# RWKV level solve: the second T1 bank is copied by VectorE, the first by ScalarE

## The chip, the cores and the metric

The kernel runs on one core of one Trainium2 chip, as one launch. The metric is the device time of that launch in microseconds (us). Before the change three runs took 2896.85, 2897.07 and 2900.86 us, median 2897.07.

## The reference, cut to what matters

The program is a two-block transformer over 1024 tokens of width 1024. The second block has a mixer of which one half is an RWKV-7 recurrence of 8 heads of 64 channels, written in the reference as a scan over tokens:

```
def step(state, inp):                       # state: (heads, 64, 64)
    r_t, w_t, k_t, v_t, a_t, b_t = inp
    sa = einsum('bhvk,bhk->bhv', state, a_t)
    state = state * w_t + sa[..., None] * b_t + v_t[..., None] * k_t
    return state, einsum('bhvk,bhk->bhv', state, r_t)
```

The kernel computes this in chunks of 64 tokens. In a chunk the term `sa` couples every token with all earlier ones; resolving this needs the inverse of a unit triangular 64x64 matrix for each head and chunk. The inverse is built by doubling: blocks of size 2, then 4, up to 64. One doubling is called a level, and there are five (`LEVELS = 5`). With X the inverse of the diagonal blocks so far and L the part of the matrix that joins neighbouring blocks, a level computes T1 = L·X and then adds X·T1 to X (and the transpose of the product to the transposed copy XT).

## The kernel before

The change is in the stage `stage_rwkv_pairs`. Heads are handled two at a time: pair c = 0..3. A pair has 8 tiles of 128 tokens, that is 16 chunks, for each of its two heads j = 0, 1. One head's 16 chunk matrices of 64x64 lie side by side in one PSUM bank of 128x512.

All engines follow one list of steps, `script`, each through its own function of the same name. For a pair c it is: `turn`, `A`, `AV`, then `level 1` to `level 5`, then `tail`. Behind level m comes at times a `fill` (a piece of an unrelated projection on TensorE, behind some of the levels 2 to 4 of pairs 1 to 3), and then a step of the front of the next pair: behind level 1 `proj r`, behind level 2 `proj k`, behind level 3 `proj v`, behind level 4 `small`, behind level 5 `sums`. The last pair has no such steps, only fills. Nothing is reordered: each engine works through its own functions in this order.

A level on the engines:

- TensorE: T1 for j = 0 and then j = 1 (L1836), 64 instructions in all, into two banks of `ringA`. Then for each j it waits until that T1 bank has been copied, and multiplies it with XT (L1844, L1847) into one or two banks of `ringD`. Level 5 has the second product only.
- ScalarE: copies both T1 banks into SBUF, j = 0 and then j = 1 (L2208). In the profile the tile T1 is named LX.
- VectorE: adds the products to Xm (L2353) and XT (L2356), in the order Xm0, XT0, Xm1, XT1.

`small` of the next pair turns two small products of TensorE (L1768) into decay and gate: ScalarE applies four sigmoids and a square (L2138, L2143), VectorE a chain of seven operations with a scan (L2282 to L2292). `sums`: TensorE multiplies the squares of ScalarE with a matrix of ones (L1777); ScalarE takes the root (L2150) and then exponentials (L2152 to L2155); VectorE takes the maximum with 1e-12, the reciprocal and further products (L2302 to L2318), with the adds of the tail (L2365, L2369) among them; its last operation writes `at`. `tail` uses the finished XT in TensorE's products L1869 and others. The next pair's `turn` needs `at` and k of this front: TensorE's second group of transposes (L1789, of k) waits for it.

A ring is a set of four PSUM banks with two counting semaphores, `full` and `free`. TensorE takes banks in a fixed order and waits until `free` has counted the use four banks earlier. Counting works only if the banks are given back in the order in which they were taken.

Of the kernel before, what the change touches and what calls it, by code (L numbers as in the profile page):

```python
# [857 lines left out]
class Forget:  # L858
# [49 lines left out]
    def biased(self, dve, link):  # L908
        V, ring, of = self.nc.vector, self.ring, self.set
        link(dve, V.memset(self.one, 1.0))  # L910
        for hf in range(NH):
            dve.wait_ge(ring.full, ring.nth(("f", hf)))
            V.tensor_scalar(self.z[:, hf * HALF:(hf + 1) * HALF], ring.bank(("f", hf))[0:FOX_HEADS, :], self.E.b_forget[:], None,
                            ALU.add).then_inc(ring.free, 1)
        dve.wait_ge(ring.free, ring.nth(("f", NH - 1)))
        V.tensor_scalar(self.low, self.z, 0.0, None, ALU.min).then_inc(of["logit"], 1)

    def sums(self, dve, link):
        V, of = self.nc.vector, self.set
        dve.wait_ge(of["logit"], 1)  # L920
        dve.wait_ge(of["log"], 1)

        link(dve, V.tensor_tensor(self.e, self.e, self.low, ALU.subtract))
        V.tensor_tensor_scan(self.z, self.one, self.e, 0.0, ALU.mult, ALU.add).then_inc(of["ncum"], 1)
# [571 lines left out]
LEVELS = 5  # L1496
# [115 lines left out]
def stage_rwkv_pairs(nc, E, A):  # L1612
# [13 lines left out]
    with ExitStack() as st:  # L1626
        NW = 2
        split = slice(IN_THREE[0], ND)
        w, w_lo = [], []
# [30 lines left out]
        h_hi = [E.sb("h_hi0", [P, S], F32R, ctx=st)]  # L1660
# [5 lines left out]
        abT, akT, rbT, rkT, Xm, XT, T1 = (E.sb(x, [P, 2, W], ctx=st) for x in ("abT", "akT", "rbT", "rkT", "Xm", "XT", "LX"))  # L1666
# [5 lines left out]
        ringA = Ring(E.banks[0:4], E.sem("rwA_full"), E.sem("rwA_free"))  # L1672
        ringD = Ring(E.banks[4:8], E.sem("rwD_full"), E.sem("rwD_free"))
# [7 lines left out]
        router_landed = E.sem("router_landed")  # L1681
        modT, modT_set, mod_moved = E.sb("modT", [2 * ND, P], ctx=st), E.sem("modT_set"), E.sem("mod_rows_moved")
        uv_landed, uv_stored = E.sem("w_uv_landed"), [E.sem(f"uv_stored{i}") for i in range(2)]
        S_ = {x: E.sem("rw_" + x) for x in ("rest", "kept", "sq", "cc", "front", "level", "exp1", "exp2", "exp3", "stored", "tanh", "rstore", "ab", "h_hi", "h_lo", "w_hi", "w_lo", "u_hi", "u_lo")}
        w_in = A["w_in_2"][0].rearrange("(c p) n -> p c n", p=P)
        win = w_in[:, :, 2 * GW:]
        KIND = "rkv"
# [11 lines left out]
        front = [("proj", "r"), ("proj", "k"), ("proj", "v"), ("small",), ("sums",)]  # L1699
# [22 lines left out]
        with nc.Block() as block:  # L1722

            @block.tensor
            def _(pe):
                def take(ring, key):
                    bank, free = ring.take(key)
                    wait(pe, ring.free, free)
                    return bank
# [13 lines left out]
                def proj(c, kind):  # L1743
                    m = 3 * c + KIND.index(kind)
                    pe.wait_ge(w_landed[m % NW], 16 * (m // NW + 1))
                    for hf in range(NH):
# [3 lines left out]
                        if hf == 0:  # L1750
                            pe.wait_ge(S_["w_lo"], m + 1)
                        if m == 0:
                            pe.wait_ge(S_["h_lo"], len(IN_THREE) * (hf + 1))
                        for i, d in enumerate(IN_THREE):
# [6 lines left out]
                def small_(c):  # L1761
                    pe.wait_ge(ringD.free, ringD.nth(("lora", 0, 1)))
                    pe.wait_ge(S_["tanh"], 1)
                    pe.wait_ge(small, 16 * E.n_small)
# [6 lines left out]
                def sums(c):  # L1771
                    if c == 0:
                        pe.wait_ge(masks_set, E.n_masks)
                    pe.wait_ge(S_["sq"], c + 1)
                    for hf in range(NH):
# [3 lines left out]
                def turn(c):  # L1779
                    for x, src in (("v", v), ("k", k), ("b", bt), ("a", at)):  # L1780
                        if x == "v":
                            pe.wait_ge(ringD.free, ringD.nth(("v", c, 1)))
                        if x == "k":
                            pe.wait_ge(S_["front"], c + 1)
                        for hf in range(NH):
# [13 lines left out]
                def fill_(*at_):  # L1799
                    for _ in range(fill.get(at_, 0)):  # L1800
# [6 lines left out]
                        if t == 0:  # L1807
                            pe.wait_ge(S_["u_lo"], q + 1)
                        for i, d in enumerate(IN_THREE):
# [20 lines left out]
                def level(c, m):  # L1830
                    for j in range(2):
                        pe.wait_ge(S_["level"], 2 * (LEVELS * c + m - 1) + j + 1)
                        pe.wait_ge(ringD.free, ringD.nth(("X", c, j) if m == 1 else ("dXT", c, m - 1, j)))
                        bank = take(ringA, ("T1", c, m, j))
                        for t, rows in chunks:
                            last = nc.tensor.matmul(bank[rows, of(t)], L[other(rows), m - 1, j, of(t)], Xm[other(rows), j, of(t)], start=True, stop=True)  # L1836
                        last.then_inc(ringA.full, 1)
                    for j in range(2):
                        pe.wait_ge(ringA.free, ringA.nth(("T1", c, m, j)))
                        to_X = take(ringD, ("dX", c, m, j)) if m < LEVELS else None  # L1840
                        to_XT = take(ringD, ("dXT", c, m, j))
                        for t, rows in chunks:
                            if m < LEVELS:
                                last_X = nc.tensor.matmul(to_X[other(rows), of(t)], XT[rows, j, of(t)], T1[rows, j, of(t)], start=True, stop=True)  # L1844
                                if t == NT - 1 and rows.start:
                                    last_X.then_inc(ringD.full, 1)
                            last = nc.tensor.matmul(to_XT[rows, of(t)], T1[rows, j, of(t)], XT[rows, j, of(t)], start=True, stop=True)  # L1847
                        last.then_inc(ringD.full, 1)
# [10 lines left out]
                def tail(c):  # L1859
# [43 lines left out]
                    for t in range(NT):  # L1903
                        for q, rows, j, o in of_tiles:
# [3 lines left out]
                    fill_("Yi", c)  # L1908

                steps = {"lora": lora, "proj": proj, "small": small_, "sums": sums, "turn": turn, "A": a_part, "AV": av, "level": level, "tail": tail,  # L1910
                         "fill": fill_}
                for name, *args in script:
# [166 lines left out]
            def _(act):  # L2079
                def got(key):  # L2080
                    act.wait_ge(ringA.full, ringA.nth(key))
                    return ringA.bank(key)
# [117 lines left out]
                        nc.scalar.copy(aAV[:, j, :, HD:2 * HD], bank.rearrange("p (t n) -> p t n", t=NT)).then_inc(ringA.free, 1)  # L2200

                def level(c, m):
                    for j in range(2):
                        bank = got(("T1", c, m, j))
                        if not (c == 0 and m == 1):
                            before = (c, m - 1) if m > 1 else (c - 1, LEVELS)
                            act.wait_ge(ringD.full, ringD.nth(("dXT", before[0], before[1], j)))
                        nc.scalar.copy(T1[:, j, :], bank[:]).then_inc(ringA.free, 1)  # L2208

                def tail(c):  # L2210
                    for j in range(2):
# [17 lines left out]
            def _(dve):  # L2229
# [116 lines left out]

                def level(c, m):
                    V = nc.vector
                    for j in range(2):
                        if m < LEVELS:  # L2350
                            key = ("dX", c, m, j)
                            dve.wait_ge(ringD.full, ringD.nth(key))
                            V.tensor_tensor(Xm[:, j, :], Xm[:, j, :], ringD.bank(key)[:], ALU.add).then_inc(ringD.free, 1)  # L2353
                        key = ("dXT", c, m, j)
                        dve.wait_ge(ringD.full, ringD.nth(key))
                        V.tensor_tensor(XT[:, j, :], XT[:, j, :], ringD.bank(key)[:], ALU.add).then_inc(ringD.free, 1)  # L2356
# [1264 lines left out]
def build_program(nc, A):  # L3621
    with ExitStack() as ctx:
# [97 lines left out]
        with ExitStack() as second:  # L3720
            E.w_hi = [E.sb(f"wr_hi{i}", [P, len(IN_THREE), P], F32R, ctx=second) for i in range(2)]
            E.uv_hi = E.sb("uv_hi", [P, len(IN_THREE), UVW], F32R, ctx=second)
            E.sb("w_lora_rest", [P, ND * (2 * LORA + GATE_LORA) - len(IN_THREE) * (2 * P + UVW)], ctx=second)
            E.bonus = E.sb("bonus", [P, NT, 2 * NPAIR], ctx=second)
            E.carry = E.sb("carry", [P, NPAIR, NC], ctx=second)
            E.ident2 = E.sb("ident2", [P, HD], ctx=second)
            E.xg = E.sb("xg", [GATE_LORA, S], ctx=second)
            E.rw = E.sb("rw", [P, ND, N_GROUPS + EXPERTS], ctx=second)
            E.rb = E.sb("rb", [P, N_GROUPS + EXPERTS], ctx=second)
            E.hT = E.xT  # L3730
            with ExitStack() as ahead:
                E.w_o = E.sb("w_o", [P, ND, D], ctx=ahead)
                E.ws = E.sb("ws", [P, GW // HD, P], ctx=ahead)
                E.gln_w, E.gln_b = (E.sb(x, [P, 512], ctx=ahead) for x in ("gln_w", "gln_b"))
                E.g2 = E.sb("g2", [GATE_LORA, RW], ctx=ahead)
                E.bs = E.sb("bs", [P, GW // HD], ctx=ahead)
            E.run(stage_rwkv_pairs, A)
            modulated.close()
            E.run(stage_mix, A, x2_rows, x3_rows, n3_rows, y_slots)
# [39 lines left out]
```

## Time and profile before

| | |
|---|---|
| median of three runs | 2897.07 us |
| the profiled execution | 2900.66 us, of which the span from the first to the last instruction is 2898.9 us |
| TensorE busy | 2780.6 us, 96% of the span |
| VectorE, ScalarE, GpSimd busy | 1764.8, 1278.9 and 561.5 us |
| mean granted TensorE clock | 0.987 of full speed |
| the level steps of the stage | from 1604.6 to 1990.4 us of the span |

TensorE is the busiest engine over the whole program, but what one step is worth is read from the stretch in which it runs: which wait ends last there. In the timelines, an engine's idle time ahead of an operation stands in brackets with what ended it; "issue" means that the profile shows no releaser.

### The profile page before, as it was taken

What the parts mean: (1) busy time and instruction counts of PE and PEld (TensorE: products, weight loads), DVE (VectorE), ACT (ScalarE), POOL (GpSimd) and SP (SyncE); (2) the same over time, 40 slices, a digit from 0 to 9 for tenths busy, and PEclk for the clock granted to TensorE, in tenths of its full rate; (3) what the DMA queues carried; (4) which work ended last, traced back from release to release, by engine and by line L of the source; (5) the groups of instructions that cost most, each with busy time, mean ns of one, the idle gap of its engine ahead of it and who ended that gap; (6) DMA issues with size and microseconds to landing.
All of it is one profiled execution on the core that took longest, in us unless ns stands there. A gap on an engine that the chain in (4) does not pass through costs nothing. (4 is left out here: it accounts for less than half of the span.)

```text
span 2898.9 us, 48471 instructions
## 1 busy us (share of the span) xinstructions
PE 2780.6 (96%) x19821; PEld 2178.4 (75%) x19821; DVE 1764.8 (61%) x2546; ACT 1278.9 (44%) x2069; POOL 561.5 (19%) x383
## 2 busy tenths in 40 slices
PE   8999999999999999999999999998799899999997
PEld 6877767777777777776766676778678788888884
DVE  2332263686565566666435364363885899999996
ACT  2111020222454444544224233232443788888883
POOL 2222232131222222222230110110000111111102
PEclk9999999999999999999999999999899999999999
DMA  5111121663211222213121021124573899999997
GB/s 178 41 40 47 67 80 65 194 215 124 66 54 57 59 59 59 59 44 117 66 79 37 28 70 31 62 66 155 175 237 146 321 390 398 402 395 393 396 387 293
DMA packets 232145, 445.61 MB, mean 154 GB/s; under 512 B 18256, under 2 KB 160096, under 8 KB 206608
## 3 DMA queue, kind: packets, MB, share of 16 engines
q1 hardware_dynamic: 224896, 426.07, 41.4%
q0 software_dynamic: 7056, 16.79, 1.6%
q8 instruction: 142, 2.33, 0.3%
q14 instruction: 51, 0.42, 0.0%
HBM read 389.78 MB, written 61.94 MB: 156 GB/s over the span
## 5 line engine op out<-in xcount | busy, mean ns | idle before, releaser
L1223 DVE TENSOR_TENSOR fox_pT_lo<-psum,fox_pT_hi 128x512 fp32r<-128x512 f32 (+2 forms) x192 | 107.1, 558 | 180.2 <-ACT fox_pT_hi L1162 170.6
L1030 PE MATMUL psum<-x_hi,w_hi 128*128 128x512 f32 x512 | 210.7, 412 | 2.3 <-PEq L100 1.7
L1032 PE MATMUL psum<-x_hi,w_lo 128*128 128x512 f32 x512 | 200.9, 392 | 0.0
L1031 PE MATMUL psum<-x_lo,w_hi 128*128 128x512 f32 x512 | 200.2, 391 | 0.0
L3237 POOL DMA_INDIRECT xg<-n_rows,idx x33 | 84.5, 2562 | 476.2 <-PE psum L3124 454.3
L3347 DVE TENSOR_TENSOR lo_g<-land_g,hi_g 128x2048 fp32r<-128x2048 f32 x68 | 152.8, 2288 | 16.8 <-ACT hi_g L3273 16.8
L1173 ACT ACTIVATE fox_p<-fox_p,fox_bias 128x256 f32<-128x256 f32 (+7 forms) x128 | 99.6, 778 | 118.4 <-DVE fox_bias L1209 115.1
L3347 DVE TENSOR_TENSOR lo_u<-land_u,hi_u 128x2048 fp32r<-128x2048 f32 x66 | 150.6, 2285 | 0.0
L3347 DVE TENSOR_TENSOR lo_d<-land_d,hi_d 128x2048 fp32r<-128x2048 f32 x64 | 143.7, 2289 | 0.0
L181 PE MATMUL psum<-x_hi,w_hi 128*128 128x512 f32 x352 | 138.4, 393 | 0.0
L182 PE MATMUL psum<-x_lo,w_hi 128*128 128x512 f32 x352 | 137.9, 392 | 0.0
L183 PE MATMUL psum<-x_hi,w_lo 128*128 128x512 f32 x352 | 137.6, 391 | 0.0
L730 PE MATMUL psum<-wo_hi,y_hi 128*128 128x512 f32 x320 | 131.5, 411 | 0.0
L2075 POOL TENSOR_TENSOR L<-abT,m_level 128x512 f32<-128x512 f32 x40 | 56.1, 1434 | 377.6 <-ACT abT L2192 377.1
L1749 PE MATMUL psum<-hT,wr 128*128 128x512 f32 x288 | 127.9, 593 | 0.0
L3273 ACT CAST hi_g<-land_g 128x2048 fp32r<-128x2048 f32 x68 | 126.1, 1903 | 2.4 <-DMA land_g<-in_moe_w_gate 2.4
L1162 ACT CAST fox_pT_hi<-psum 128x512 fp32r<-128x512 f32 (+2 forms) x192 | 86.0, 483 | 92.3 <-PE psum L1058 92.3
L1135 POOL CAST w_hi<-w_land 128x1024 fp32r<-128x1024 f32 x46 | 47.7, 1037 | 399.9 <-PE psum L1032 317.6
L731 PE MATMUL psum<-wo_lo,y_hi 128*128 128x512 f32 x320 | 125.1, 391 | 0.0
L732 PE MATMUL psum<-wo_hi,yT_lo 128*128 128x512 f32 x320 | 124.7, 390 | 0.0
L3273 ACT CAST hi_u<-land_u 128x2048 fp32r<-128x2048 f32 x66 | 122.4, 1903 | 1.0 <-DMA land_u<-in_moe_w_up 1.0
L3273 ACT CAST hi_d<-land_d 128x2048 fp32r<-128x2048 f32 x64 | 118.8, 1905 | 5.7 <-PE psum L3131 5.5
(582 smaller groups left out, 7407.7 us busy)
## 6 DMA issues: line engine op xcount, KB each, us to landing
land_g<-in_moe_w_gate SPq DMA_DIRECT2D x66, 1024.0 KB, 7.3
land_u<-in_moe_w_up SPq DMA_DIRECT2D x66, 1024.0 KB, 7.2
land_d<-in_moe_w_down SPq DMA_DIRECT2D x64, 1024.0 KB, 8.2
ada<-in_ada_w SPq DMA_DIRECT2D x24, 1024.0 KB, 5.3
y_slots<-yb SPq DMA_DIRECT2D x33, 512.0 KB, 9.3
w<-in_w_in SPq DMA_DIRECT2D x27, 512.0 KB, 4.0
wo<-in_w_out SPq DMA_DIRECT2D x12, 1024.0 KB, 10.7
w_land<-in_w_kv_shared SPq DMA_DIRECT2D x23, 512.0 KB, 4.1
```

What stands on the lines that cost most here:

```text
L181: self.nc.tensor.matmul(bank[:], hi[:, d, :], E.x_hi[:, d, cols], start=(d == 0), stop=False)
L182: self.nc.tensor.matmul(bank[:], hi[:, d, :], E.x_lo[:, d, cols], start=False, stop=False)
L183: last = self.nc.tensor.matmul(bank[:], lo[:, d, :], E.x_hi[:, d, cols], start=False, stop=(d == ND - 1))
L730: nc.tensor.matmul(bank, hi, w_hi, start=first, stop=False)
L731: nc.tensor.matmul(bank, hi, wo_lo[:, c, cols], start=False, stop=False)
L732: last = nc.tensor.matmul(bank, E.y_lo[:, c, rows], w_hi, start=False, stop=final)
L1030: nc.tensor.matmul(bank[:], hi[:, d, :], E.x_hi[:, d, cols], start=(d == 0), stop=False)
L1031: nc.tensor.matmul(bank[:], hi[:, d, :], E.x_lo[:, d, cols], start=False, stop=False)
L1032: last = nc.tensor.matmul(bank[:], lo[:, d, :], E.x_hi[:, d, cols], start=False, stop=(d == ND - 1))
L1749: nc.tensor.matmul(bank[:], w[m % NW][:, d, :], E.hT[:, d, cols], start=(d == 0), stop=False)
L3273: nc.scalar.copy(w_hi[kept_in(x, b)][:], land[kept_in(x, b)][:]).then_inc(hi_set[x], 1)
L3347: V.tensor_tensor(w_lo[kept_in(x, b)][:], land[kept_in(x, b)][:], w_hi[kept_in(x, b)][:].bitcast(F32), ALU.subtract).then_inc(lo_set[x], 1)
```

## The change

ScalarE copies T1 of j = 0 only. VectorE copies T1 of j = 1, as the first operation of its own `level` function, and counts it in a new semaphore `T1`. The bank of j = 1 is given back by VectorE, after it has waited until ScalarE gave back that of j = 0, so that the order holds. ScalarE ends its `level` with a wait for that. TensorE waits for the new semaphore ahead of the products of j = 1.

```diff
@@ TensorE, level(c, m) @@
                     for j in range(2):
-                        pe.wait_ge(ringA.free, ringA.nth(("T1", c, m, j)))
+                        if j == 0:
+                            pe.wait_ge(ringA.free, ringA.nth(("T1", c, m, 0)))
+                        else:
+                            pe.wait_ge(S_["T1"], LEVELS * c + m)
@@ ScalarE, level(c, m) @@
-                    for j in range(2):
-                        bank = got(("T1", c, m, j))
-                        if not (c == 0 and m == 1):
-                            before = (c, m - 1) if m > 1 else (c - 1, LEVELS)
-                            act.wait_ge(ringD.full, ringD.nth(("dXT", before[0], before[1], j)))
-                        nc.scalar.copy(T1[:, j, :], bank[:]).then_inc(ringA.free, 1)
+                    bank = got(("T1", c, m, 0))
+                    if not (c == 0 and m == 1):
+                        before = (c, m - 1) if m > 1 else (c - 1, LEVELS)
+                        act.wait_ge(ringD.full, ringD.nth(("dXT", before[0], before[1], 0)))
+                    nc.scalar.copy(T1[:, 0, :], bank[:]).then_inc(ringA.free, 1)
+                    act.wait_ge(ringA.free, ringA.nth(("T1", c, m, 1)))
@@ VectorE, level(c, m) @@
                     V = nc.vector
+                    dve.wait_ge(ringA.full, ringA.nth(("T1", c, m, 1)))
+                    V.tensor_copy(T1[:, 1, :], ringA.bank(("T1", c, m, 1))[:]).then_inc(S_["T1"], 1)
+                    dve.wait_ge(ringA.free, ringA.nth(("T1", c, m, 0)))
+                    dve.wait_ge(S_["T1"], LEVELS * c + m)
+                    dve.sem_inc(ringA.free, 1)
                     for j in range(2):
                         if m < LEVELS:
                             key = ("dX", c, m, j)
```

The new semaphore is also added to the table `S_` at the head of the stage.

## Rows read from the trace of the kernel before

**Rows 1.** Busy time by stretch: us; PE, PEld, DVE, ACT, POOL busy; PEclk; DMA.
```profile
1627.00:1661.00 34.00, 34.00 (x448) 20.75 (x442) 8.89 (x16) 5.65 (x10) 0.00 (x0) 1.00 0.11 31
1661.00:1700.00 39.00, 34.70 (x816) 29.84 (x810) 31.21 (x30) 21.08 (x35) 0.00 (x0) 1.00 0.22 75
```

**Rows 2.** What TensorE waited for, 1603 to 1992: total us, times, longest us.
```profile
PE psum L1789 <- DVE at L2318: 3.9, 3, 1.3
PE psum L1847 <- issue: 3.9, 3, 2.4
PE psum L1847 <- ACT LX L2208: 3.2, 3, 1.1
PE psum L1869 <- issue: 2.5, 3, 0.8
...
PE psum L1836 <- issue: 1.2, 3, 0.5
...
PE psum L1856 <- issue: 1.0, 2, 0.6
...
PE psum L1844 <- issue: 0.6, 1, 0.6
```

**Rows 3.** Timeline of ScalarE, pair 0, level 4 to `sums`: start, duration, operation.
```profile
1660.67 0.59 ACT L2208 COPY LX<-psum 128x512 f32<-128x512 f32 x1 [0.35 <-PE psum L1836]
...
1665.88 1.17 ACT L2143 ACTIVATE tmp<-k,rwkv_cols 128x1024 f32<-128x1024 f32 x1
1666.92 1.09 ACT L2208 COPY LX<-psum 128x512 f32<-128x512 f32 x2
1671.64 1.28 ACT L2150 ACT_TABLE_LOAD   x1 [3.64 <-PE psum L1777]
```

**Rows 4.** Timeline of ScalarE, the same wait in pairs 1 and 2.
```profile
1792.71 1.28 ACT L2150 ACT_TABLE_LOAD   x1 [3.64 <-PE psum L1777]
...
1913.90 1.28 ACT L2150 ACT_TABLE_LOAD   x1 [3.64 <-PE psum L1777]
```

**Rows 5.** Timeline of VectorE, pair 0, from `small` to the end of `sums`.
```profile
1665.53 0.70 DVE L2282 TENSOR_SCALAR lw<-lw 128x1024 f32<-128x1024 f32 x1 [1.42 <-ACT lw L2138]
...
1670.48 1.22 DVE L2292 TENSOR_TENSOR lw<-cl,lw 128x1024 f32<-128x1024 f32 x1
1671.62 1.28 DVE L2356 TENSOR_TENSOR XT<-XT,psum 128x512 f32<-128x512 f32 x2
1674.16 0.69 DVE L2302 TENSOR_SCALAR tmp<-tmp 128x1024 f32<-128x1024 f32 x1 [1.26 <-ACT tmp L2150]
1674.89 6.55 DVE L2303 RECIPROCAL tmp<-tmp 128x1024 f32<-128x1024 f32 x1
...
1693.66 1.22 DVE L2318 SCALAR_TENSOR_TENSOR at<-at,lw 128x1024 f32<-128x1024 f32 x1
```

**Rows 6.** Timeline of VectorE, level 5's adds in pairs 1 and 2.
```profile
1792.68 1.28 DVE L2356 TENSOR_TENSOR XT<-XT,psum 128x512 f32<-128x512 f32 x2
...
1913.88 1.28 DVE L2356 TENSOR_TENSOR XT<-XT,psum 128x512 f32<-128x512 f32 x2
```

**Rows 7.** Timelines of TensorE, pair 0: level 5's products, `sums`, the tail, the next `turn`.
```profile
1667.57 0.62 PE L1847 MATMUL psum<-XT,LX 64*64 64x64 f32 x14 [1.08 <-ACT LX L2208]
...
1669.58 1.13 PE L1777 MATMUL psum<-tmp,blocksum 128*128 128x512 f32 x2
...
1672.40 0.33 PE L1869 MATMUL psum<-aAV,XT 64*64 64x128 f32 x2 [0.84 <-issue]
...
1694.94 0.33 PE L1789 MATMUL psum<-ident,k 128*128 128x128 f32 x1 [1.31 <-DVE at L2318]
```

**Rows 8.** VectorE's copies of one PSUM bank elsewhere, 0 to 60 us, by form.
```profile
L261 DVE COPY x0T<-psum 128x512 f32<-128x512 f32 x8 | 5.5, 692 | 6.3 <-PE psum L252 6.3
```

**Rows 9.** Timeline of TensorE, pair 3, level 1: the longest idle time of the levels.
```profile
1961.76 0.21 PE L1847 MATMUL psum<-XT,LX 64*64 64x64 f32 x1 [2.38 <-issue]
```

**Rows 10.** Busy time of TensorE by stretch, pair 3: us, busy, PEclk.
```profile
1959.00:1962.00 3.00, 0.62 (x42) 1.00 0.13 45
1962.86:1966.27 3.41, 3.25 (x80) 0.50 0.02 5
```

**Rows 11.** Busy time of all engines, pair 3: T1 of level 2, T1 of level 4.
```profile
1963.89:1966.81 2.92, 2.92 (x63) 2.92 (x65) 1.16 (x2) 0.59 (x1) 0.00 (x0) 0.59 0.02 6
1978.28:1980.12 1.84, 1.84 (x63) 1.84 (x65) 0.00 (x0) 0.96 (x2) 0.00 (x0) 1.00 0.25 77
```

**Rows 12.** Timeline of VectorE, pair 3, level 2 and level 5.
```profile
1968.08 0.69 DVE L2353 TENSOR_TENSOR Xm<-Xm,psum 128x512 f32<-128x512 f32 x1 [3.03 <-PE psum L1844]
...
1988.82 0.69 DVE L2356 TENSOR_TENSOR XT<-XT,psum 128x512 f32<-128x512 f32 x1 [4.98 <-PE psum L1847]
```

**Rows 13.** Timeline of ScalarE, pair 3, the second copies of level 2 and level 5.
```profile
1967.11 0.59 ACT L2208 COPY LX<-psum 128x512 f32<-128x512 f32 x1 [0.57 <-PE psum L1836]
...
1987.92 0.59 ACT L2208 COPY LX<-psum 128x512 f32<-128x512 f32 x1 [0.35 <-PE psum L1836]
```

More of the change, by code:

```diff
@@ L1683, in stage_rwkv_pairs @@
         uv_landed, uv_stored = E.sem("w_uv_landed"), [E.sem(f"uv_stored{i}") for i in range(2)]
-        S_ = {x: E.sem("rw_" + x) for x in ("rest", "kept", "sq", "cc", "front", "level", "exp1", "exp2", "exp3", "stored", "tanh", "rstore", "ab", "h_hi", "h_lo", "w_hi", "w_lo", "u_hi", "u_lo")}
+        S_ = {x: E.sem("rw_" + x) for x in ("rest", "kept", "sq", "cc", "front", "level", "exp1", "exp2", "exp3", "stored", "tanh", "rstore", "ab", "T1", "h_hi", "h_lo", "w_hi", "w_lo", "u_hi", "u_lo")}
         w_in = A["w_in_2"][0].rearrange("(c p) n -> p c n", p=P)
```

## The prediction

> **What bounds the kernel now.** I read the busy time by stretch first. In levels 2 to 4 of pair 0 TensorE is busy for all of 34.00 us; in the stretch from level 5 to the next `turn` it is busy for 34.70 of 39.00 us, and VectorE for 31.21 [rows 1]. So the levels themselves are bound by TensorE, and only around level 5 do other engines hold it up. The waits of TensorE say by what: 3.2 us in three times for ScalarE's copy of T1 in level 5, 2.5 us at L1869 without a named releaser, and 3.9 us at L1789 for `at`, VectorE's last result of `sums` [rows 2]. Three times is once for each of pairs 0 to 2, which are the pairs that have a front of the next pair beside them.
>
> The timelines show the chain in pair 0. ScalarE has the sigmoids and the square of `small` ahead of level 5's copies, which start at 1666.92 [rows 3]; TensorE gets the first one at 1667.57, runs the products of both heads until 1669.58, and then `sums` [rows 7]. ScalarE waits 3.64 us for `sums` and starts the root at 1671.64 [rows 3]. VectorE takes that result at 1674.16 and has no idle time of note from there to the end of `at` at 1693.66 + 1.22 = 1694.88 [rows 5], and TensorE's transposes of k start 0.06 later, after 1.31 us of idle time [rows 7]. Hence from 1669.58 on the path is: `sums` on TensorE, root on ScalarE, a chain of 20.7 us on VectorE, the next pair's `turn`. Whatever delays `sums` delays the pair by as much. In pairs 1 and 2 ScalarE's wait for `sums` has the same 3.64 us [rows 4].
>
> The point that decides is what VectorE does meanwhile. It begins `small` at 1665.53 and ends it at 1670.48 + 1.22 = 1671.70; the two adds of level 5, for which TensorE was done at 1669.58, start only at 1671.62 [rows 5, 7]. Today nobody but the tail waits for them: L1869 starts at 1672.40, 0.10 after the first add ends (1671.62 + 0.68, from a pair of 1.28), which explains its 0.84 us without a releaser [rows 7].
>
> **The change, part by part.** *Removed from ScalarE:* 20 copies of 0.59 us. In the levels where nothing stands ahead of them the second copy starts after a wait of 0.35 us for TensorE [rows 3]: ScalarE was not late, and TensorE works on the products of head 0 meanwhile. Gain there: zero. In level 5 the two copies run back to back (1.09 us), but TensorE has 1.0 us of products of head 0 before it needs the second one [rows 3, 7]. Gain zero too.
>
> *Added to VectorE:* 20 copies out of PSUM. The same form elsewhere takes 0.69 us [rows 8], 0.1 us more than ScalarE's. In 17 of 20 levels VectorE is idle when T1 is full. The tightest that I found is level 2 of pair 3: a copy from 1967.11 ends at 1967.80, some 0.2 us of semaphore steps follow (an estimate, twice the 0.1 us hand-over above), and the next add is due at 1968.08 [rows 12, 13]; it fits. In level 5 of pair 3 the copy ends at 1988.61 and the add due at 1988.82 may slip by 0.1 [rows 12, 13]. All 17 together: 0 to 0.5 us, taken as 0.1.
>
> *Level 5 of pairs 0 to 2.* Here the copy stands behind `small` in VectorE's order. It can't start before 1671.62, where the first add starts now [rows 5]. It ends at 1671.62 + 0.69 = 1672.31, and 0.10 later, at 1672.41, TensorE has it. TensorE has finished head 0's products at 1667.57 + 1.00 = 1668.57 (half of the 2.01 us from 1667.57 to 1669.58 [rows 7]) and stands for 3.84 us, with `sums` queued behind the waiting products. Then 1.00 us for head 1's products: `sums` starts at 1673.41 and not at 1669.58, 3.83 us later. In pairs 1 and 2 the adds start at 1792.68 and 1913.88, 0.03 and 0.02 before the root's table load [rows 4, 6]; in pair 0 it was also 0.02, so the shift is the same. Three times 3.83 = 11.5 us.
>
> Is any of it hidden? VectorE: between the adds and L2302 it idles 1.26 us for the root [rows 5], and this wait moves with the root, so nothing is taken up. ScalarE's new wait at the end of `level` holds the root's table load, but that waits for `sums` anyway. The exponentials and the tail's copies move with the root by the same 3.8 us; TensorE has 1.31 us of slack against `at` [rows 7], and by that much the tail may slip further without cost. L1869 itself moves only from 1672.40 to 1675.4, since the first add is then long over. In the other levels ScalarE's new wait costs nothing where a long idle time follows; after level 4 of pair 0 it moves the next table load by some 0.2 us.
>
> *The clock.* A stall of 3.84 us is longer than any in the levels now. The longest is 2.38 us, in level 1 of pair 3, [rows 9], with TensorE busy for 0.62 of the 3.00 us around it; soon after it the granted clock stood at 0.50, that is 1.2 instead of 2.4 GHz, for 3.41 us [rows 10]. Under it the T1 products of level 2 took 2.92 us, against 1.84 in level 4 at full clock [rows 11]: 1.08 us lost. The waits of today around level 5, 1.08 and 0.84 us, left the clock at 1.00 [rows 1, 7]. I expect that most of the new stalls drop it, just when head 1's products and `sums`, 3.0 us of work, are on the path. Bounds for each stall: 0 (no drop) and 1.7 us (all of 3.41 us on the path at half the speed). I take the row, 1.08, for each of three: 3.2 us; three times the bounds give 0 and 5.1.
>
> The Trainium skill ("TensorE: Matmul & The Clock Gate", section "Terms") prices throttled time at its length times (1 − K/N), a half at K=4 of N=8. By that rule and the 3.41 us row three drops would cost 5.1 us and the sum would be 16.7; the trace gives less, 1.08 us in the 2.92 us of the row above, of which some was back at full clock, so the measured price stays in the sum.
>
> **The sum.** 11.5 + 3.2 + 0.1 = 14.8 us. On the profiled execution's own time, 2900.66 us (span 2898.9 and 1.8 around it), this gives 2915.5. That execution is 3.6 us above the median of the runs, 2897.07, so the time to compare is 2897.1 + 14.8 = 2911.9 us.
>
> **The rivals.**
> 1. *The stalls come, the clock stays.* 2897.1 + 11.6 = 2908.7 us. For it: the mean clock of the stretch is 1.00 today with two shorter waits in it. Against: a stall of only 2.38 us was followed by a drop.
> 2. *Not slower: the stops in TensorE's instruction supply go away.* Several waits of TensorE have no releaser: 3.9 us at L1847, 1.2 at L1836, 1.0 at L1856, 0.6 at L1844 [rows 2], 6.7 us in all, plus the clock drop of 1.1 behind the longest. If they depend on how the instruction stream meets other work, new timing could remove them, at most 7.8 us, and 14.8 − 7.8 = 7.0 still is slower; without the clock's 3.2 it is 3.8, or 2900.9 us, which counts as no change. It decides from 11.6 − 5.8 = 5.8 us saved, nearly all of it, and with no clock drop. Nothing in the change aims at them, and a gap longer than they are is added.
> 3. *More is lost: the second copy is late in the other levels as well.* If VectorE's copy and its semaphore steps delayed the adds of pair 3, where no front hides them, by the 0.1 us difference of the copies plus some 0.2, in 5 levels, and the clock drops cost their upper bound, the sum is 11.5 + 5.1 + 1.5 = 18.1: 2915.2 us. For it: the fit in level 2 of pair 3 is tight [rows 12, 13].
> 4. *The delay is hidden anyway:* if the `sums` chain had slack, only the L1869 path would count, 3.0 us less the 1.31 of slack, times three = 5.1: 2902.2 us. Against: TensorE waits for `at` three times, the full length of the chain [rows 2, 5].
>
> **Chances and range.** Forecast (with two or three clock drops, 2909 to 2914) 0.55; rival 1, or one drop, 0.22; rival 2 0.05; rival 3 0.10; rival 4 0.05; else 0.03. What a measurement of this kernel tells from no change is about 0.2%, 5.8 us: slower means above 2902.9. Slower 0.91, the same 0.07, faster 0.02. The range is 2903 to 2917: from just under rival 1 with part of rival 2, up to rival 3 and its 2 us of run spread. The likeliest case's own range is 2909 to 2914.
>
> **What the changed profile would show.** VectorE's copy of T1 in level 5 starts at the end of L2292, and not when L1836 is done; TensorE shows a wait of about 3.8 us for it at L1847, three times; the wait of L1869 is gone; ScalarE waits some 7.4 us instead of 3.64 for L1777; the wait of L1789 for `at` stays near 1.3 us, as both its sides move together. Stretches at clock 0.50 appear around 1673, and one turn of pairs later twice more. In the levels 1 to 4 nothing moves by more than 0.2 us. I am wrong if TensorE's wait in level 5 is under 3 us, if the wait for `at` shrinks to zero (then the tail is the path), or if the time between one pair's level 1 and the next one's grows by less than 3 us.

## The result, and the profile after

Three runs of the changed kernel took 2915.57, 2922.14 and 2925.05 us, median 2922.14, against 2897.07 before: 25.1 us more, where 14.8 were forecast, and above the top of the range, 2917. The ratios given here and below, with their 95% intervals, are estimates from the runs and not quotients of the two medians: here 1.0071 (1.0058 to 1.0085), that is 20.6 us (16.8 to 24.6), where the medians' quotient is 1.0087. In a later session five more runs of the changed kernel had the median 2922.32 and fifteen of the kernel before 2900.53: 21.8 us more by the medians, ratio 1.0066 (1.0052 to 1.0079), that is 19.1 us (15.1 to 22.9). So some 3 us of the surprise was a low median of the three runs before. The rest, 7 us by the medians, was a real error; even the lower end of the interval is above 14.8. Where a difference is given in us below, it is one of medians.

The profiled execution took 2922.14 us; its span is 2920.4, 21.5 us longer than before. First, what TensorE waited for in the stage (total us, times, longest us), to be set beside [rows 2]:

```profile
PE psum L1850 <- DVE LX L2353: 10.9, 3, 3.6
PE psum L1850 <- issue: 4.4, 3, 2.1
PE psum L1789 <- DVE at L2321: 3.9, 3, 1.3
PE psum L1850 <- ACT LX L2210: 3.2, 3, 1.1
PE psum L1883 <- ACT GH L2219: 2.7, 4, 0.7
PE psum L1836 <- ACT lw L2141: 2.7, 3, 1.3
```

The first line is new: three waits of 3.6 us for VectorE's copy (now L2353). The wait for `at` is the same 3.9 us as before. That is the sign of a delay ahead of a chain which is not absorbed by it. The last line is one that was not forecast: 2.7 us and three times, where the kernel before had 1.3 us and two.

VectorE in pair 0, from `small` to `sums` (start, duration), beside [rows 5]:

```profile
1668.06 0.69 DVE L2285 TENSOR_SCALAR lw<-lw 128x1024 f32<-128x1024 f32 x1 [2.84 <-ACT lw L2141]
...
1673.00 1.22 DVE L2295 TENSOR_TENSOR lw<-cl,lw 128x1024 f32<-128x1024 f32 x1
1674.15 0.68 DVE L2353 COPY LX<-psum 128x512 f32<-128x512 f32 x1
1674.96 0.69 DVE L2364 TENSOR_TENSOR XT<-XT,psum 128x512 f32<-128x512 f32 x1
1676.90 0.69 DVE L2364 TENSOR_TENSOR XT<-XT,psum 128x512 f32<-128x512 f32 x1 [1.25 <-PE psum L1850]
1682.75 0.69 DVE L2305 TENSOR_SCALAR tmp<-tmp 128x1024 f32<-128x1024 f32 x1 [5.16 <-ACT tmp L2153]
```

The copy starts where the chain of `small` ends, as the prediction put it. From the first line to the last are 14.69 us; before, 8.63 (1665.53 to 1674.16). TensorE's side, from two stretches of its timeline, and ScalarE's wait for `sums`, beside [rows 3, 7]:

```profile
1674.88 0.48 PE L1850 MATMUL psum<-XT,LX 64*64 64x64 f32 x4 [3.64 <-DVE LX L2353]
...
1676.78 1.22 PE L1777 MATMUL psum<-tmp,blocksum 128*128 128x512 f32 x1
```
```profile
1664.81 1.28 ACT L2141 ACT_TABLE_LOAD   x1 [3.38 <-PE psum L1768]
...
1680.23 1.28 ACT L2153 ACT_TABLE_LOAD   x1 [10.19 <-PE psum L1777]
```

Head 1's products take 1.90 us, from 1674.88 to 1676.78, and not 1.00, and ScalarE gets the result of `sums` 3.45 us after that, not 2.06. The granted clock says why (us, TensorE busy, PEclk):

```profile
1672.00:1676.00 4.00, 1.12 (x20) 0.59 0.00 0
1676.00:1680.00 4.00, 4.00 (x21) 0.55 0.00 0
1680.00:1684.00 4.00, 3.76 (x41) 1.00 0.02 4
1802.00:1806.00 4.00, 3.57 (x34) 0.57 0.00 0
1928.50:1935.50 7.00, 5.98 (x40) 0.52 0.00 0
```

TensorE was at 1.2 instead of 2.4 GHz around the end of every one of the three stalls, for some 7, 3.5 and 7 us. In pair 0 the lower clock begins at about 1672.5, 2.4 us before the stall ends; in pairs 1 and 2 it begins 0.2 and 1.0 us before.

To see where the 21.5 us arise I compare the starts of the same operations in both timelines. In each pair, "level 1" is ScalarE's first copy of T1, "small" VectorE's first operation of `small`, "root" its first operation of `sums`. A number says by how many us the distance between two of them grew over the kernel before. The other columns are the experiments below.

| step | changed | again | lv14 | lv5 | warm | wide | early | split | square |
|---|---|---|---|---|---|---|---|---|---|
| pair 0, level 1 to small | 3.53 | 1.83 | 1.29 | 0.01 | 3.53 | 1.84 | 3.52 | 0.51 | -0.01 |
| pair 0, small to root | 6.06 | 6.50 | 0.31 | 5.81 | 3.87 | 3.87 | -1.35 | 6.03 | -1.03 |
| root to level 1 of pair 1 | -0.05 | -0.01 | -0.01 | -0.01 | 0.40 | 0.10 | 0.62 | 0.09 | 0.01 |
| pair 1, level 1 to small | 0.48 | 0.39 | 0.40 | 0.24 | 0.39 | 0.74 | 2.43 | 0.45 | 0.21 |
| pair 1, small to root | 5.43 | 5.80 | -0.01 | 5.41 | 3.88 | 3.87 | -1.36 | 5.37 | -1.03 |
| root to level 1 of pair 2 | 0.07 | 0.15 | 0.07 | 0.01 | 1.77 | -0.18 | 0.77 | 0.07 | 0.06 |
| pair 2, level 1 to small | 0.39 | 0.38 | 0.48 | 0.00 | 5.13 | 0.39 | 2.01 | 0.41 | 0.00 |
| pair 2, small to root | 6.49 | 6.50 | -0.01 | 5.24 | 3.87 | 3.87 | -1.36 | 6.49 | -1.03 |

In the changed kernel the three steps from small to root make up 18.0 us, the other steps of the table 4.4 us. The stage starts 1.0 us earlier in this execution and pair 3 and what follows differ by 0.1, which gives the 21.5 us.

### The profile page after: what moved, and what is told of

The parts are those of the page before. It is cut to its first block and busy times, and to the rows that moved or that the text cites. A ratio compares the mean times of both kernels' runs of the same rounds, so it can differ in the third digit from the quotient of the medians.

```text
span 2920.4 us, 48478 instructions
## 1 busy us (share of the span) xinstructions
PE 2789.4 (96%) x19821; PEld 2183.4 (75%) x19821; DVE 1777.2 (61%) x2566; ACT 1267.8 (43%) x2049; POOL 561.7 (19%) x383
## 5 line engine op out<-in xcount | busy, mean ns | idle before, releaser
L3355 DVE TENSOR_TENSOR lo_g<-land_g,hi_g 128x2048 fp32r<-128x2048 f32 x68 | 152.8, 2288 | 16.8 <-ACT hi_g L3281 16.8
```

The costliest lines, as they stand in the source:

```text
L3355: V.tensor_tensor(w_lo[kept_in(x, b)][:], land[kept_in(x, b)][:], w_hi[kept_in(x, b)][:].bitcast(F32), ALU.subtract).then_inc(lo_set[x], 1)
```

## The experiments

**again.** The changed kernel unaltered, timed five times.

> The changed kernel once more, unaltered, as the measure for the runs beside it. Both theories: about 22 us above the kernel before (2915 to 2925 us), and about the same again here; its scatter shows how much of the difference is steady.

2922.32 us (2916.69 to 2924.51) against 2900.53: ratio 1.0066 (1.0052 to 1.0079). The difference is steady; single runs scatter over 8 us.

**lv14 and lv5.** The same edit in part of the levels. In all three functions of `level` the new branch is taken for the levels in a list only (written here against the changed kernel, ScalarE's part alone; the marks ... stand for lines left out):

```diff
+        ON_V = (1, 2, 3, 4)          # lv5: (5,)
+        nth_v = lambda c, m: len(ON_V) * c + ON_V.index(m) + 1
...
-                    bank = got(("T1", c, m, 0))
+                    for j in range(1 if m in ON_V else 2):
+                        bank = got(("T1", c, m, j))
...
-                    act.wait_ge(ringA.free, ringA.nth(("T1", c, m, 1)))
+                    if m in ON_V:
+                        act.wait_ge(ringA.free, ringA.nth(("T1", c, m, 1)))
```

> VectorE copies the second T1 in levels 1 to 4 only; level 5 is left to ScalarE as before. Theory A (VectorE's order in level 5 costs the time): the three stalls and their clock drops go, what stays is the sigmoid table load of pair 0 behind its wait (1.4 us) and 0.1 us for each of 16 levels (a copy of 0.69 for one of 0.59 us): 2.5 to 3.5 us above before, 2900 us. Theory B (the hand-over in every level costs it): 16 of 20 levels keep it, so 80% of 22 us stays: 2915 us.

2902.80 us over eleven runs: ratio 1.0010 (1.0001 to 1.0019), 2.3 us.

> VectorE copies the second T1 in level 5 only; levels 1 to 4 are as before. Theory A: the stalls of TensorE stay at 3.6 us three times and cost 18 us with the clock drops: 2915 us, and the table load of pair 0 runs early as in the kernel before. Theory B: only 4 of 20 levels, 20% of 22 us: 2901 us.

2918.07 us: ratio 1.0052 (1.0038 to 1.0066), 17.5 us. Theory B fell: 16 of the 20 hand-overs cost a tenth of the loss, the 4 of level 5 cost 80% of it. In lv5 TensorE waits for the copy three times 3.6 us again, and VectorE in pair 0 makes it behind `small`, so the stall needs level 5 alone:

```profile
1667.76 1.23 DVE L2299 TENSOR_TENSOR lw<-cl,lw 128x1024 f32<-128x1024 f32 x1
1668.90 0.68 DVE L2358 COPY LX<-psum 128x512 f32<-128x512 f32 x1
```

**warm and wide.** VectorE's copy comes as late as before, but TensorE is kept at work while it waits. The line marked warm is in warm alone; the line marked wide and the three below it are in wide alone:

```diff
                         else:
+                            if m == LEVELS and c + 1 < NPAIR:
+                                keep_warm(nc, E, pe, ringD, 15)                     # warm
+                                spare, free = ringD.next()                          # wide
+                                wait(pe, ringD.free, free)
+                                for _ in range(3):
+                                    nc.tensor.matmul(spare[:], E.ident[:], tok["v"][:, 0:4, :], start=True, stop=True)
                             pe.wait_ge(S_["T1"], LEVELS * c + m)
```

> The changed kernel with 15 matmuls of a 128x128 unit matrix, into a free bank, between the products of head 0 and the wait for VectorE's copy in level 5 of pairs 0 to 2 (some 3.4 us of work in a stall of 3.6). Theory A1 (a good third of the level 5 cost is the granted clock falling behind an idle TensorE): no stretch at 0.50 behind the stalls, 5 to 7 us faster than the changed kernel. Theory A2 (the stall alone costs it, and the drops fall where they do for other reasons): the same time as the changed kernel or slower by up to 1 us.

2925.05 us, ratio 1.0080 (1.0066 to 1.0094), 2.7 us above the changed kernel beside it: by the total, A1 failed. The 2.7 us lie within the two intervals. By the table A1 was right in its place: the steps from small to root are 3.87, 3.88 and 3.87 us, and the clock was 1.00 there. The time was lost elsewhere, in the profiled execution 1.8 + 5.1 us around level 1 of pair 2. There TensorE shows waits without a releaser; from 1700 to 1930 us they are these in warm, and in the changed kernel (again) there are none of 0.2 us or more in the same stretch:

```profile
PE psum L1852 <- issue: 3.9, 3, 2.1
...
PE psum L1893 <- issue: 1.2, 1, 1.2
PE psum L1806 <- issue: 0.9, 1, 0.9
PE psum L1789 <- issue: 0.8, 1, 0.8
...
PE psum L1825 <- issue: 0.6, 1, 0.6
```

> The changed kernel with 3 matmuls of 128x512 (some 3 us of work in few instructions) in each of the three stalls, in place of the 15 of 128x128 tried before. Theory C (there the clock's gain of 6 to 7 us in level 5 was real and was lost again to stops of TensorE without a releaser, because 90 more instructions shift where they fall): the stretches at 0.50 behind the stalls are gone, the steps from small to root are 3.9 us each, no new stops in pairs 1 and 2: 5 to 7 us faster than the changed kernel, 2916 us. Theory D (TensorE kept busy costs as much as the clock gives back): 2922 us or more, with the steps at 3.9 us and the loss elsewhere again.

2915.36 us, ratio 1.0038 (1.0024 to 1.0052), 7.0 us faster than the changed kernel in again, and 6.6 us faster than split, which was timed beside it. The steps from small to root are again 3.87 us, the five like waits are gone, and the clock held (us, TensorE busy, PEclk):

```profile
1671.00:1675.00 4.00, 2.93 (x43) 1.00 0.01 4
1675.00:1679.00 4.00, 3.13 (x37) 1.00 0.00 0
1679.00:1683.00 4.00, 3.76 (x39) 1.00 0.00 0
```

TensorE in wide, pair 0. The products of head 1 and `sums` take 1.08 and 1.98 us again, although TensorE still waits for the same copy:

```profile
1672.26 1.15 PE L1855 MATMUL psum<-XT,LX 64*64 64x64 f32 x32 [1.07 <-ACT LX L2215]
1673.34 2.84 PE L1846 MATMUL psum<-tok_v,ident 128*128 128x512 f32 x6
1677.05 1.15 PE L1855 MATMUL psum<-XT,LX 64*64 64x64 f32 x32 [0.87 <-DVE LX L2358]
1678.13 1.98 PE L1777 MATMUL psum<-tmp,blocksum 128*128 128x512 f32 x4
```

So theory C holds for the clock. That warm's loss comes from its number of instructions fits both runs, but what stops TensorE there was not tried by itself.

**early.** The same copy, at another place in VectorE's order:

```diff
                 def small_(c):
                     V = nc.vector
+                    if c > 0:
+                        second_T1(c - 1, LEVELS)      # wait for T1 of j = 1, copy it, count it
...
-                    dve.wait_ge(ringA.full, ringA.nth(("T1", c, m, 1)))
-                    V.tensor_copy(T1[:, 1, :], ringA.bank(("T1", c, m, 1))[:]).then_inc(S_["T1"], 1)
+                    if m < LEVELS or c + 1 == NPAIR:
+                        second_T1(c, m)
```

> The changed kernel, but VectorE makes the level 5 copy of pairs 0 to 2 ahead of `small` in its order, not behind it. Theory A (the place in VectorE's order is what costs, not the copy): TensorE's wait for the copy goes from 3.6 us to zero three times, no clock drop follows, and VectorE's `small` starts some 1.5 us later, of which about 0.5 us reaches the root's result: step from small to root about +0.5 us against the kernel before in each pair; with the table load (1.3) and 0.1 us a level 4 to 5 us above before, about 2903 us. Theory B (the copy or its semaphores cost wherever they stand): 2915 us or more.

2904.86 us over eleven runs, ratio 1.0013 (1.0004 to 1.0022), 4.4 us. The hand-over is whole, but 17 of 22 us are gone, so it is the place in the order that costs. The three waits of 3.6 us are gone from TensorE's list; what leads it now is a wait of the tail (total us, times, longest us):

```profile
PE psum L1872 <- ACT tmp L2153: 7.7, 3, 2.8
PE psum L1850 <- issue: 4.1, 4, 2.4
```

The profile names ScalarE, but the times point to VectorE. TensorE's tail starts 0.10 us after VectorE's first add of XT ends (1672.10 + 0.68), and so it does in pairs 1 and 2 (1795.64 and 1918.25, with adds that end at 1795.54 and 1918.15); it is the same 0.10 that the prediction read at L1869 [rows 5, 7]. The adds still stand behind `small`:

```profile
1672.88 3.11 PE L1872 MATMUL psum<-aAV,XT 64*64 64x128 f32 x32 [2.83 <-ACT tmp L2153]
1672.10 1.28 DVE L2370 TENSOR_TENSOR XT<-XT,psum 128x512 f32<-128x512 f32 x2
```

"No clock drop follows" did not hold. Behind each of these three waits (2.83, 2.44 and 2.43 us) the granted clock stood at 0.50 for some 3.5 us:

```profile
1673.40:1676.90 3.50, 3.50 (x29) 0.52 0.02 5
1796.25:1799.75 3.50, 3.50 (x29) 0.52 0.02 5
1919.10:1922.60 3.50, 3.50 (x25) 0.53 0.02 5
```


VectorE in pair 0 makes the copy first and starts `small` behind it:

```profile
1665.42 0.69 DVE L2280 COPY LX<-psum 128x512 f32<-128x512 f32 x1 [4.74 <-PE psum L1836]
1666.02 0.68 DVE L2291 TENSOR_SCALAR lw<-lw 128x1024 f32<-128x1024 f32 x1
```

The expected start of `small` 1.5 us later shows in the table as 2.0 and 1.6 in pairs 1 and 2 (2.43 and 2.01, less the 0.4 of their levels). Less 1.36 from small to root this leaves 0.7 and 0.3 us, where 0.5 was expected. A further 0.6 to 0.8 us comes behind the root and was not expected. There the tail has become the path: TensorE's wait for `at`, 3.9 us before and in the changed kernel, is missing from its list. The late adds and the half clock behind them are both in that tail; no run parts the two.

**split.** One column copied on ScalarE behind the new wait at the end of level 4 of pair 0:

```diff
                     act.wait_ge(ringA.free, ringA.nth(("T1", c, m, 1)))
+                    if (c, m) == (0, 4):
+                        nc.scalar.copy(apart[:, 0:1], E.ident[:, 0:1])
```

> The changed kernel with a copy of one column on ScalarE behind the new wait at the end of level 4 of pair 0, so that this wait isn't merged with those of the sigmoid. Theory E (the new wait pushes the wait for the small product ahead of the sigmoid's table load): the table load starts right behind level 4, TensorE's wait of 1.3 us at L1836 falls to 0 in pair 0, 1.3 us faster than the changed kernel (2920 to 2921 us). Otherwise: no difference.

2921.93 us, ratio 1.0069 (1.0056 to 1.0083): by the total no difference from the changed kernel (0.4 us less) can be told. The trace shows it: the table load starts at 1662.70 and no longer behind a wait for L1768, TensorE's waits at this place fall from 2.7 to 1.4 us in all, and the step from level 1 to small is 0.51 us, against 1.83 in again. ScalarE in split:

```profile
1660.66 0.59 ACT L2211 COPY LX<-psum 128x512 f32<-128x512 f32 x1 [0.40 <-PE psum L1837]
1662.36 0.19 ACT L2214 COPY apart<-ident 128x1 f32<-128x1 f32 x1 [1.12 <-DVEq L2359]
1662.70 1.28 ACT L2142 ACT_TABLE_LOAD   x1
1664.59 0.69 ACT L2142 ACTIVATE lw<-psum,rwkv_cols 128x512 f32<-128x512 f32 x1 [0.61 <-PE psum L1769]
```

The traces show where the load stands, not the waits themselves; these were read in the compiled programs. In that of the changed kernel the wait for the product of `small` and a wait for the front are merged into one instruction, which stands ahead of the load; the new wait took its place at the sigmoid. Without the new wait it is the product's that stands at the sigmoid, behind the load.

**square.** No part of the change; it acts on the same path from the other end. In the kernel before, ScalarE's square moves behind the copies of level 5:

```diff
+                    if c == 0:
+                        square(c)
+
+                def square(c):
                     act.wait_ge(ringD.free, ringD.nth(("k", c, 1)))
...
                         nc.scalar.copy(T1[:, j, :], bank[:]).then_inc(ringA.free, 1)
+                    if m == LEVELS and c + 1 < NPAIR:
+                        square(c + 1)
```

> The kernel before (ScalarE makes both copies), with ScalarE's square of `small` (1.17 us) moved behind the level 5 copies of pairs 0 to 2. If the start of `sums` is what the path hangs on, as the stall of the changed kernel says, the copies come 1.04 us earlier, TensorE's wait of 1.08 us for them is gone, and each pair is 1.0 us shorter: 3 us faster than the kernel before. If VectorE's `small` sets the path instead: no difference.

2896.22 us over eleven runs against 2900.42 over 21: ratio 0.9987 (0.9978 to 0.9996), 4.2 us faster by the medians, where 3 were expected; 3.1 are in the table (three times 1.03). TensorE's waits of 1.1 us for the level 5 copies are missing from its list. It is faster than both kernels. ScalarE in pair 0: both copies now start right behind the sigmoids, and the wait for `sums` shrinks from 3.64 to 2.44 us:

```profile
1667.84 1.24 ACT L2212 COPY LX<-psum 128x512 f32<-128x512 f32 x2
1668.97 1.15 ACT L2147 ACTIVATE tmp<-k,rwkv_cols 128x1024 f32<-128x1024 f32 x1
1672.57 1.28 ACT L2154 ACT_TABLE_LOAD   x1 [2.44 <-PE psum L1777]
```

## Why the prediction was wrong

The direction, the place and the main term were right; three smaller terms were too low, by a factor of two or more each.

- *The stall, 11.5 us.* Right. With the clock held, warm and wide show 3.87 us in each pair, 11.6 in all, against 3.83. Also right: nothing hides it, and the wait for `at` stays at 3.9 us. early shows that the order is the cause.
- *The clock, 3.2 us.* This is the step that failed. The steps from small to root exceed 3.87 by 2.19, 1.56 and 2.62 us in the changed kernel, 6.4 in all, and by 7.2 in again; wide gains 7.0 us by holding the clock. The price of one drop, 1.08 us, was taken from T1 products of 64x64 over a stretch that was in part at full clock. Here the lower clock meets the two products of 128x512 as well, and twice it lasted some 7 us, so that two of the three drops cost more than even the upper bound of 1.7 us. By the rule of the Trainium skill that the prediction quoted ("TensorE: Matmul & The Clock Gate", "Terms"), about 17 us at half clock would be 8.5 us, as an estimate. The trace has 6.4. In it 3.6 us of these 17 pass while TensorE still stands, and half of the rest is 6.7. So with the measured length the rule was an upper bound, and nearer than the row; what the prediction lacked under either was the length of the stretches.
- *ScalarE's new wait behind level 4.* The prediction had it move the table load by 0.2 us and left it out of the sum. It cost 1.3 us in pair 0 (1.83 in again, 0.51 in split). I had looked only at how long ScalarE waits, not at what the wait does to the table load behind it.
- *The longer copies, 0.1 us for all levels.* They cost 0.1 us for each level: 0.38 to 0.48 us for the four levels of pair 1 or 2 in changed, again and lv14, against 0.24 and 0.00 in lv5, where ScalarE makes them. I had checked whether VectorE was free for its next add, and not whether TensorE waits for the copy itself. It does: in pair 0, level 4, ScalarE's second copy ends at 1661.26 [rows 3], when TensorE is just done with head 0's products, and the first copies of levels 2, 3 and 4 follow each other after 17.26 and 17.24 us in the changed kernel, after 17.18 and 17.17 before.
- *What stays.* These terms make 11.6 + 6.8 (the mean of 6.4 and 7.2) + 1.3 + 1.6 (16 levels at 0.1) = 21.3 of the 21.8 us between the medians of the later session. The 16 levels include pair 3, where waits without a releaser hide so small a term; there it is taken and not shown. In the profiled execution of the changed kernel, pair 0 has 1.7 us more from level 1 to small than again has; a stretch at half clock from 1611 to 1614.5 stands there, and again has none. Single executions differ by such drops.
- *The signs.* The copy starts at the end of `small`, the stall, the lower clock and the wait for `at` came as named. ScalarE waits 10.19, 9.56 and 10.63 us for `sums` and not 7.4: the clock is in it, and 0.5 us for the second copy that ScalarE no longer makes, which the prediction had overlooked. The levels 1 to 4 of a pair grew by 0.4 us and pair 0 by 1.3 more, and not by 0.2 at most.

Of the rivals, none was it. Rival 3 had the right sign, and its sum was the nearest, but for its clock term's bound and for another place (pair 3). Rivals 1 and 2 fell with the drops of the clock in all three stalls, rival 2 also because the waits without a releaser did not go (6.9 us in the stage against 7.1 before); rival 4 with the unchanged wait for `at`.

## What to carry to other kernels

Moving an operation to an idler engine moves it into that engine's order: look up what stands ahead of it there at the moment when its input is ready, for each place where it occurs. VectorE was less than half busy in this stage [rows 1: 8.89 of 34 us in levels 2 to 4], and still late by 5 us in 3 of 20 cases, which made four fifths of the loss (lv5: 17.5 of 21.8 us). In this kernel a stall of TensorE of 3.6 us cost itself and some 60% again for the clock (6.8 us on 11.6), so price both and not the stall alone. Look for the gain first in what stands ahead of the late operation: moving one square back gave 3 to 4 us where moving the copy away lost 22.

## What the hardware showed that I had not expected

- The clock fell around each of the three stalls of 3.5 to 3.65 us in all of changed, again, lv5 and split, and stayed at 1.2 GHz for about 3.5 or about 7 us. Some 3 us of filler in a stall, with a wait of 0.87 us left, kept it at 2.4 GHz.
- The length of a wait does not decide alone. Waits of 2.4 to 2.8 us in the tail were followed by the half clock three times of three in early, waits of 1.9 us at the same place in square never; but a wait of 1.80 us without a releaser, in level 1 of pair 0 of the changed kernel, was.
- Waits of TensorE without a releaser move with the instruction stream: 45 added 128x128 products (two instructions each in the trace) brought 7.4 us of them to a stretch that had none, and 9 wide products that fill the same time did not. Why is open.
- A wait added on ScalarE changed which waits the compiler merges, and by that whether a table load of 1.28 us runs before or after its operand is ready.
